# Squares added in pairs on VectorE ahead of one summing product, in thirteen norms of a two-block model

## The reference, cut to what matters

```
def rms_norm(x, g):
    y = xf * lax.rsqrt(jnp.mean(xf * xf, axis=-1, keepdims=True) + EPS)
    return (y * g.astype(jnp.float32)).astype(x.dtype)

def memory_cross_attention(h, m, wq, wk, wv, q_g, k_g, wo):
    q = rms_norm((h @ wq).reshape(bsz, L, XA_HEADS, XA_HEAD_DIM), q_g)   # 4 heads of 256
    k = rms_norm((m @ wk).reshape(bsz, N_MEM, XA_HEADS, XA_HEAD_DIM), k_g)
```

## Time and profile before

| | |
|---|---|
| time, median of 3 runs | 1131.88 us (1131.68 to 1132.12) |
| the profiled execution | 1135.88 us |
| its span | 1133.9 us, 20122 instructions |
| granted TensorE clock, mean | 0.993 of full speed |
| TensorE busy | 1101.8 us, 97% |
| VectorE busy | 838.0 us, 74% |
| ScalarE busy | 619.9 us, 55% |

### The profile page before, as it was taken

The page is one execution under the profiler, slowest core; times in us unless marked ns, Lnnn a source line. Parts: engine busy times, 40 slices in busy tenths (PEclk is TensorE's granted clock), DMA queues, the critical chain, the costliest instruction groups (busy, mean ns, idle before and its releaser), DMA issues.

```text
span 1133.9 us, 20122 instructions
## 1 busy us (share of the span) xinstructions
PE 1101.8 (97%) x7645; PEld 973.9 (86%) x7645; DVE 838.0 (74%) x1277; ACT 619.9 (55%) x1113; POOL 40.1 (4%) x42
## 2 busy tenths in 40 slices
PE   6999999999999999999999999999999899999997
PEld 5996778999989999999966889999988688888886
DVE  4797783656687887876467588878887867888876
ACT  6752446565564554563464555545555865545544
POOL 2000000010200000010000100000010001000000
PEclk9998999999999999999999999999999999999999
DMA  9551222352666566465420357657577146557651
GB/s 291 171 187 39 75 75 75 113 186 75 198 185 201 172 182 199 135 207 173 142 65 1 112 152 219 184 152 218 185 147 166 24 134 178 173 165 222 179 158 70
DMA packets 218591, 169.69 MB, mean 150 GB/s; under 512 B 20859, under 2 KB 208290, under 8 KB 218402
## 3 DMA queue, kind: packets, MB, share of 16 engines
q1 hardware_dynamic: 217106, 164.43, 49.5%
q0 software_dynamic: 912, 4.00, 1.2%
q10 hardware_dynamic: 512, 0.40, 0.1%
HBM read 167.76 MB, written 1.05 MB: 149 GB/s over the span
## 4 chain that ended last, share of the span: by engine, by line
PE 86%; DVE 6%; ACT 5%; issue 1%; DMA 1%; SPq 0%; ACTq 0%; DVEq 0%
PE bank L2549 20%; PE bank L2168 18%; PE bank L2097 11%; PE bank L2098 10%; PE bank L2099 10%; PE bank L2551 10%; DVE wlo L1431 2%; PE bank L2162 2%; PE bank L2163 2%; PE bank L2164 2%; DVE arena L1424 1%; ACT whi L783 1%; DMA raw<-in_w_in_dram 1%; ACT arena L1370 1%; DVE wlo L1841 1%
## 5 line engine op out<-in xcount | busy, mean ns | idle before, releaser
L2549 PE MATMUL bank<-mem_pair,whi 128*128 128x512 f32 x1056 | 375.7, 398 | 0.7 <-DVE xT L1762 0.7
L2551 PE MATMUL bank<-mem_pair,wlo 128*128 128x256 f32 x1056 | 296.4, 281 | 0.0
L2549 PEld LDWEIGHTS bank<-mem_pair,whi 128*128 128x128 f32 x1056 | 198.4, 188 | 47.6 <-issue 0.9
L2097 PE MATMUL bank<-act_hi,whi 128*128 128x256 f32 (+1 forms) x744 | 215.6, 290 | 4.0 <-DVE act_lo L1463 1.7
L1841 DVE TENSOR_TENSOR wlo<-raw,whi 128x1024 fp32r<-128x1024 f32 x177 | 208.8, 1220 | 5.4 <-ACT whi L1207 1.6
L2098 PE MATMUL bank<-act_lo,whi 128*128 128x256 f32 (+1 forms) x744 | 211.9, 285 | 0.0
L1431 DVE TENSOR_TENSOR wlo<-raw,whi 128x1024 fp32r<-128x1024 f32 (+3 forms) x137 | 162.0, 1223 | 67.4 <-ACT whi L783 66.4
L2099 PE MATMUL bank<-act_hi,wlo 128*128 128x256 f32 (+1 forms) x744 | 211.7, 285 | 0.0
L2551 PEld LDWEIGHTS bank<-mem_pair,wlo 128*128 128x128 f32 x1056 | 199.5, 189 | 0.8
L1207 ACT ACTIVATE whi<-raw 128x1024 fp32r<-128x1024 f32 x180 | 179.7, 1045 | 0.3 <-PE bank L2168 0.3
L1227 ACT ACTIVATE arena<-arena 128x256 f32<-128x256 f32 x66 | 27.6, 418 | 247.8 <-DVE arena L1424 247.8
(11 more groups left out here) (238 smaller groups left out, 1423.6 us busy)
## 6 DMA issues: line engine op xcount, KB each, us to landing
raw<-in_ffn_w_in_dram SPq DMA_DIRECT2D x132, 512.0 KB, 5.2
raw<-in_ffn_w_out_dram SPq DMA_DIRECT2D x33, 1024.0 KB, 5.1
raw<-in_w_in_ab_dram SPq DMA_DIRECT2D x11, 1024.0 KB, 6.4
raw<-in_w_in_dram SPq DMA_DIRECT2D x9, 1024.0 KB, 7.2
raw<-in_xa_wk_dram SPq DMA_DIRECT2D x4, 1024.0 KB, 5.4
raw<-in_xa_wv_dram SPq DMA_DIRECT2D x4, 1024.0 KB, 5.2
raw<-in_w_out_dram SPq DMA_DIRECT2D x4, 1024.0 KB, 5.1
raw<-in_xa_wq_dram SPq DMA_DIRECT2D x4, 1024.0 KB, 5.0
```

The lines of the kernel that those rows point to most:

```text
L2097: pe.matmul(dst, w[0], a[0], start=start, stop=False, **kw)
L2549: pe.matmul(b[:].rearrange("p (h t) -> p h t", h=2), w[0][:, k, g, :], mem_pair[:, :, k, :], start=k == 0, stop=False, skip_group_check=True)
L2551: last = pe.matmul(b[:, 0:T], w[1][:, k, g, :], mem_hi[:, k, :], start=False, stop=k == KC - 1, skip_group_check=True)
```

## The change

VectorE adds the two halves of a square buffer in place (`pair_sum`), and TensorE multiplies the ones with that one tile of 256 columns and not with two. TensorE's wait for the squares (`s_sq`) becomes a wait for the addition (`s_pair`). It is done for four key heads ("xk"), the layer norm, the three branch norms, three of the four query heads and both latent norms: thirteen places; of the norms in parts only the first part, of two tiles, is added. VectorE's additions stand at fixed places in its program: for key head h between the softplus of head h + 1 and the splits.

```
+        PAIRED = [("xk", 0), ("xk", 1), ("xk", 2), ("xk", 3), ("ln", 0), ("branch", 1), ("branch", 2), ("branch", 0), ("xq", 0), ("xq", 1), ("xq", 2), ("lat", 0), ("lat", 1)]
...
+            def pair_sum(stat):
+
+                n = SQ[stat]
+                dve.wait_ge(s_sq, n + 1)
+                dve.tensor_tensor(sq[:, n % 2, 0:T], sq[:, n % 2, 0:T], sq[:, n % 2, T:2 * T], ALU.add).then_inc(s_pair, 1)
+
             state_quarter(0, lambda: sb_softplus(0))
             sb_softplus(1)
             for h in range(4):
                 if h:
                     sb_softplus(h + 1)
                 after("xk", 2 * h)
+                pair_sum(("xk", h))
                 after("xk", 2 * h + 1)
...
             conv_centre()
+            pair_sum(("ln", 0))
             after("xv", 0)
...
             sb_softplus(7)
+            pair_sum(("branch", 1))
             ssm_product()
             after("xv", 4)
             after("xv", 5)
             dve.wait_ge(s_conv_act, 2)
+            pair_sum(("branch", 2))
             branch_scaled(0)
             branch_scaled(1)
+            pair_sum(("branch", 0))
             branch_low(0)
...
             for h in range(3):
+                pair_sum(("xq", h))
                 mean_square(("xq", h), bank[4][:, 0:T], 256)
...
+            pair_sum(("lat", 0))
             for i in range(5):
                 after("lat", i)
             mean_square(("lat", 0), bank[4][:, 0:T], 384)
+            pair_sum(("lat", 1))
...
                 n = SQ[stat] + number
-                pe.wait_ge(s_sq, n + 1)
+                if number == 0 and stat in PAIRED:
+                    tiles = 1
+                    pe.wait_ge(s_pair, PAIRED.index(stat) + 1)
+                else:
+                    pe.wait_ge(s_sq, n + 1)
```

More of the change, by code:

```diff
@@ L481, in build @@
         s_mean = sem("final_mean_square"); s_scale = sem("final_scale_ready"); s_fine = sem("final_evacuated"); s_fine2 = sem("last_half_evacuated"); s_yg = sem("final_gain_applied")
-        s_store = sem("stored")
+        s_store = sem("stored"); s_pair = sem("pair_of_squares_added")
         def ring_bank(name, idx):
```

## The result

The changed kernel takes 1150.14 us (median of 4 runs, 1149.93 to 1154.29) against 1132.0 (median of 4, 1131.68 to 1136.22) of the kernel before: ratio 1.0162, 95% interval 1.0145 to 1.018. It is 18.1 us slower. The forecast was 1146.4, between 1137.0 and 1153.5. One of the later runs of the kernel before took 2020.34 us, at a mean granted clock of 0.857; the ratios leave it out.

A forecast was written before the change was run, and what follows sets the result against it. TensorE, busy 97% of the span, was taken as the bound. Key heads +10.17, nine norms -3.22 (+6.95 together) and clock +7.5 made +14.5 on 1131.9, so 1146.4 us, range 1137.0 to 1153.5.

The forecast's parts named there:

- The stalls: Key heads 1 to 3: TensorE waits 4.13, 4.12 and 4.12 us for additions queued behind VectorE's state block and softplus.
- The addition: VectorE's sum of the two 128x256 halves in SBUF takes 0.42 us, with 0.06 for the signal to TensorE.
- Key head 0: First key head: VectorE is idle ahead of the split, TensorE waits 0.21 and is given back 0.43, net -0.22 us.
- The nine norms: Layer, branch, query and latent norms: eight save 0.43 each, branch 2 costs 0.22 after waiting 0.65; together -3.22 us.
- The clock: Behind the three key-head stalls TensorE falls to half clock, costing 0 to 15.0 us; the middle, 7.5, was taken.
- the short fall of the trace before: After TensorE idled 2.19 us, the clock was 0.5 from 26.36 to 29.78, 3.42 us; taken as likely as a lasting fall.
- the long fall: Clock at 0.50 for 10.12 us, 97.95 to 108.07, through the first two heads' scores; taken as likely as a short fall.
- The effect that a slow head shortens the next wait: Argument against rival 2: a head at low clock shortens the next wait, so the next clock fall may stay out.
- rival 2: Key heads: stalls, with low clock from each to the next key tile, 15.0 us of clock, 1153.9 us; chance 0.22.
- Full clock throughout: Rival 1: the key-head stalls happen but the clock stays full, 1138.9 us; chance 0.15.
- The rival on the other side: Rival 3: VectorE reaches the addition in time, all thirteen places pay, -5.6 us, so 1126.3; chance 0.04.

The follow-up runs named there:

- the experiment: The changed kernel with TensorE multiplying ones by ones 18 times ahead of its wait for the addition in key heads 1 to 3: 1139.67 us.

## Why the prediction was right, step by step

- *The stalls.* Forecast 4.13, 4.12, 4.12; the waits are 4.08, 4.08, 2.79, and the lengthening of the stretch from key tile to product is 4.15 in all three. The place in VectorE's program decided, as forecast. In head 3 the row of the wait alone would mislead: it is shorter only because TensorE came late itself, at half the clock.
- *The addition* takes 418 ns in the mean of 13, forecast 0.42.
- *Key head 0.* Forecast -0.22; TensorE waited 0.59, so +0.16. The forecast leaned on 2.22 us of VectorE idleness in an execution with the low clock just ahead. With the nine norms alone, profiled at full clock there, VectorE is idle for 0.40 ahead of the same split. The waits ahead of head 0's product are 0.59, 0.60 and 0.60 in the three profiles with full clock (the changed kernel and the two with products in the stalls), and none is shown in the two with the low clock (key heads alone, addition in the state block).
- *The nine norms.* Forecast -3.22, measured -3.09; the wait ahead of branch 2 was forecast at 0.65 and is 0.49.
- *The clock.* Forecast 7.5 as the middle of 0 and 15.0; it was 10.46 by the laps and 10.65 by the experiment. This is the term that was mis-sized: its 3.0 us and the 0.4 of head 0 are nearly all that lies between 1146.4 and 1150.14. The step that failed was to weigh the short fall of the trace before (3.42 us) like the long one. It also took the long fall without what stood ahead of it, an idle gap of 1.25 us on TensorE, whose row stands at the end of this document. Of the three new falls two were long, 10.2 and 13.6 us: the first ended 1.5 us ahead of the key tile at 139.66, the second 2.9 us behind the one at 162.48. The third was 3.4. That the forecast came within 3.7 us owes something to luck, since a middle between two bounds says nothing of how long a fall lasts. The effect that a slow head shortens the next wait was there, but only in head 3, and even 2.79 was enough.
- The Trainium skill ("TensorE: Matmul & The Clock Gate", section on HAM oscillation) has a wait in each iteration throw the clock back in each iteration. The trace agrees, three times of three; the full price that rival 2 gave it (15.0) it did not reach. Of the two waits of 1.85 us with half the products, which are shorter than those of its example, one was followed by the low clock and one was not.
- *The rivals.* Full clock throughout (1138.9) did not happen by itself, but is what came when TensorE was kept at work: 1139.67. The rival on the other side named the right point, the addition 4 us earlier, and promised -5.6 in all. With the addition there the four key heads still gave nothing: I had priced a product at its full 0.43 in a lap that VectorE bounds as much as TensorE. At neither of the two places tried did the key heads get faster.

## What to carry to other kernels

Before work is moved from one engine to another, look at where in the other engine's program it will stand when the first one needs it, not at how idle the other is: 0.42 us of work on an engine that is idle for a quarter of the time made a stall of 4.1, because a block of 10 us stood ahead of it. A stall of TensorE of some four microseconds is to be priced twice, once for itself and once for the clock behind it: the three of the changed kernel (4.08, 4.08 and 2.79) cost 3.99, 4.98 and 1.49 us of clock. Where a stall can't be avoided, products that compute nothing in its place can pay: here 54 of them gave back 10.65 us.

## What the runs showed of the hardware that was not expected

- A granted clock of 0.50 was kept from 128.0 to 138.2 us and from 151.8 to 165.4, though from 129.59 on in the first and throughout the second TensorE had no idle time: most of its products were narrow (64 or 32 rows), and at the end of the second it was in key tiles. The same kinds of products from 128 to 136 us in the kernel before kept 1.00, and the last of the 24 products from 133.44 on ran at 1.00 again, from 138.2. What ends such a stretch isn't shown.
- Two waits, of 1.85 and 1.84 us, in one execution, with like work around them, and the clock fell behind the first alone.
- The two groups of executions, 4 us apart, go with the clock ahead of the key heads. In five of the ten profiles (before, key heads alone, each of the two single late additions, addition in the state block) it falls between 98 and 101 us, behind a gap of 1.22 to 2.07 us in the convolution's products; in the other five it doesn't, and the gap is there too, 1.15 to 1.25 us. The same gap of 1.25 in the kernel before and in the changed one, the first followed by the low clock and the second not:

```profile
95.90 3.60 PE L2168 MATMUL bank<-arena 32*32 32x256 f32 x28 [1.25 <-issue]
```

```profile
96.84 2.87 PE L2184 MATMUL bank<-arena 32*32 32x256 f32 x28 [1.25 <-issue]
```

  The view could name no releaser for the gap, and what makes it was not looked into. The runs with half the products in the stalls and with one late addition in head 3 spread over 6.6 and 6.4 us and show no such two groups.
